# Expert slots' token numbers through a table in memory, and two other edits in the last pair of a one-layer diffusion backbone

## The reference, cut to what matters

```python
def hierarchical_moe(h, w_gr, b_gr, w_er, b_er, w_gate, w_up, w_down):
    ...
    e_val, e_idx = lax.top_k(e_in, TOP_K)                       # TOP_K = 2
    w_sel = jax.nn.softmax(e_val, axis=-1) * p_group
    ...
    y = jnp.zeros_like(h)
    for e in range(N_EXPERTS):                                  # 16 experts, hidden width 512
        he = jax.nn.silu(h @ w_gate[e]) * (h @ w_up[e])
        y = y + combine[:, e:e + 1] * (he @ w_down[e])
    return y
...
x = x + mod[5] * y.reshape(x.shape)
return rmsnorm(x, g_final)
```

## Time and profile before

| | us |
|---|---|
| median of 3 executions | 724.5 |
| lowest, highest | 723.94, 724.51 |
| the profiled execution, its own time | 724.15 |
| its span in the profile | 722.4 |

### The profile page before, as it was taken

One profiled execution on the slowest core, in us unless ns is written; L12 is line 12 of the kernel. 1 busy time (PEld: TensorE's weight loads), 2 busy tenths in 40 slices (PEclk: granted clock), 3 DMA queues, 4 the chain that ended last, 5 costly groups with the idle time before them and its releaser, 6 DMA issues.

```text
span 722.4 us, 7996 instructions
## 1 busy us (share of the span) xinstructions
PE 701.3 (97%) x3282; PEld 416.7 (58%) x3282; DVE 296.9 (41%) x507; ACT 112.2 (16%) x197; POOL 172.6 (24%) x126
## 2 busy tenths in 40 slices
PE   9999999999999999998999999999999999999995
PEld 5444586555775467776777788647434434443431
DVE  3439492778310475644343223325413212211315
ACT  4021011111000422221122230013000000000012
POOL 0008989789179000800000000000000000000010
PEclk9999999999999999999999999998999999999998
DMA  8994526762442332433481235995899999999991
GB/s 355 421 377 193 200 108 235 290 220 68 175 140 94 116 117 73 161 116 117 183 342 60 71 122 200 421 401 212 336 416 423 420 423 421 422 420 423 420 396 66
DMA packets 28933, 183.70 MB, mean 254 GB/s; under 512 B 3479, under 2 KB 5911, under 8 KB 13536
## 3 DMA queue, kind: packets, MB, share of 16 engines
q1 hardware_dynamic: 26880, 178.45, 62.4%
q0 software_dynamic: 1584, 3.97, 1.4%
q10 hardware_dynamic: 432, 0.75, 0.3%
HBM read 178.14 MB, written 6.82 MB: 256 GB/s over the span
## 4 chain that ended last, share of the span: by engine, by line
PE 91%; DMA 3%; DVE 2%; issue 2%; ACT 1%; SPq 0%; ACTq 0%; DVEq 0%; POOLq 0%
PE bank L1163 21%; PE bank L773 18%; PE bank L777 10%; PE bank L769 8%; PE bank L790 6%; PE bank L1116 4%; PE bank L995 4%; PE bank L796 4%; PE bank L920 2%; PE bank L941 2%; PE bank L822 2%; PE bank L928 2%; PE bank L783 2%; DMA y_rows<-sb,token_rows 1%; DMA sb<-y_rows 1%
## 5 line engine op out<-in xcount | busy, mean ns | idle before, releaser
L1163 PE MATMUL bank<-sb 128*64 128x512 f32 x768 | 167.5, 594 | 0.0
L773 PE MATMUL bank<-sb 128*128 128x256 f32 x576 | 128.5, 382 | 0.6 <-PE bank L769 0.3
L773 PEld LDWEIGHTS bank<-sb 128*128 128x128 f32 x576 | 108.1, 190 | 17.8 <-issue 3.8
L1163 PEld LDWEIGHTS bank<-sb 128*64 128x64 f32 x768 | 54.2, 137 | 106.7 <-issue 105.7
L565 POOL DMA_INDIRECT y_rows<-sb,token_rows x7 | 7.0, 997 | 371.5 <-DVE sb L1722 371.5
L525 POOL TENSOR_TENSOR sb<-sb 128x1024 f32<-128x1024 f32 x32 | 68.1, 2129 | 59.3 <-DMA sb<-ada_w 38.0
L1354 DVE COPY sb<-bank 128x512 f32<-128x512 f32 x45 | 29.2, 685 | 103.6 <-PE bank L928 66.2
L777 PE MATMUL bank<-sb 128*128 128x512 f32 x160 | 70.2, 593 | 0.3 <-PE bank L773 0.3
L769 PE MATMUL bank<-sb 128*128 128x512 f32 x128 | 55.8, 593 | 0.3 <-PE bank L995 0.3
L777 PEld LDWEIGHTS bank<-sb 128*128 128x128 f32 x160 | 29.9, 190 | 35.3 <-issue 35.3
L1687 DVE TENSOR_TENSOR sb<-sb,bank 128x512 f32<-128x512 f32 x8 | 5.5, 687 | 99.5 <-PE bank L1163 99.5
(11 more groups left out here) (246 smaller groups left out, 684.2 us busy)
## 6 DMA issues: line engine op xcount, KB each, us to landing
sb<-expert_w SPq DMA_DIRECT2D x94, 1024.0 KB, 19.3
sb<-front_w SPq DMA_DIRECT2D x19, 2048.0 KB, 8.1
sb<-ada_w SPq DMA_DIRECT2D x32, 512.0 KB, 3.5
sb<-ada_mix SPq DMA_DIRECT2D x4, 2048.0 KB, 20.4
sb<-xcT SPq DMA_DIRECT2D x4, 512.0 KB, 6.2
sb<-front_w SPq DMA_DIRECT2D x4, 512.0 KB, 21.1
y_rows<-sb SPq DMA_DIRECT2D x4, 512.0 KB, 23.2
sb<-expert_w SPq DMA_DIRECT2D x4, 512.0 KB, 5.6
```

What stands on the lines that cost most here:

```text
L773: ins = pe.matmul(ps[:, c * L:(c + 1) * L], lhs(w, k, (2 * i + c) * P), hT[:, k, 0:L], start=(k == 0), stop=(k == KD - 1))
L1163: ins = pe.matmul(bank[e * CAP:(e + 1) * CAP, :], lhsT[:, k, e * CAP:(e + 1) * CAP], weights_at(k, e), start=(k == 0), stop=(k == parts - 1))
```

## The change

**Token numbers by a table.** `tokens_of_slots` and `rows_of_tokens` are gone. In memory there is now a table `slot_tokens` of 896 integers, 7 for each of 128 partitions. DVE fills `token_rows` with 1024 at the very start, and POOL writes it out to the table. DVE works out, for each token and each of its two choices, the place of its slot in the table (`table_rows`, four columns; a place beyond the table if the choice has no slot there) and the number to be stored (`token_ids`). POOL then issues four indirect transfers of 128 single integers each, waits for them, reads the table back into `token_rows` and waits for that, all ahead of its loop over pairs. The constants `first_slot` and `token` are changed to match.

**Useless matmuls dropped.** `stay_warm` and its three uses are gone.

**The last pair's first half ahead of the rows.** On DVE, `experts_out(LAST, (0,))` now stands before all four `gathered_back` steps (it stood behind three of them), and `experts_out(LAST, (1,))` stands before `scaled_tokens` (it stood behind).

```diff
+            table = d["slot_tokens"].rearrange("(p n) o -> p (n o)", n=LAST)
+            pool.wait_ge(rows_unused, 1)
+            pool.dma_start(table, token_rows[:, :]).then_inc(table_cleared, 16)
+            pool.wait_ge(ids_ready, 2)
+            pool.wait_ge(table_rows_ready, 1)
+            pool.wait_ge(table_cleared, 16)
+            for q in range(2 * NT):
+                pool.indirect_dma_start(d["slot_tokens"][:, :], bass.IndirectOffsetOnAxis(table_rows[:, q:q + 1], 0),
+                                        token_ids[:, q:q + 1], None, bounds_check=STORED - 1, oob_is_err=False)\
+                    .then_inc(table_filled, 16)
+            pool.wait_ge(table_filled, 16 * 2 * NT)
+            pool.dma_start(token_rows[:, :], table).then_inc(token_rows_in, 16)
+            pool.wait_ge(token_rows_in, 16)
             pool.wait_ge(rows_cleared, 16 * 2 * NT)
             for n in range(LAST):
-                pool.wait_ge(token_rows_ready, 2 * n + 2)
                 pool.wait_ge(y_out, 2 * n + 2)
...
                     if q is not None and k % 4 == 0:
-                        if q == 6 * LAST + 2:
-                            stay_warm(1)
                         take_half(q + k // 4)
...
                 up(n, ring(6 * n + 2), 6 * n + 2)
                 if n < LAST:
-                    tokens_of_slots(n, S_now[n % 2])
-                if n < LAST:
                     gather(n + 1, S_now[(n + 1) % 2], (0,))
...
-                    if n == LAST and i == 0:
-                        stay_warm(2)
                     down(n, i, ring(6 * n + 4 + i), 6 * n + 4 + i)
...
+            dve.memset(token_rows[:, :], 1024).then_inc(rows_unused, 1)
             dve.memset(zeros, 0.0)
...
-                dve.scalar_tensor_tensor(out=token_of, in0=oh2, scalar=float(L),
-                                         in1=sm("token").unsqueeze(2).broadcast_to([P, NT, NE]), op0=ALU.mult, op1=ALU.add)\
-                   .then_inc(token_of_ready, 1)
+                link(dve.scalar_tensor_tensor(out=table_at, in0=slot_ok, scalar=-4096.0, in1=slot_at, op0=ALU.mult, op1=ALU.add))
+                dve.tensor_scalar(table_rows[:, :], table_at, 4096.0, None, ALU.add).then_inc(table_rows_ready, 1)
+                for j in range(2):
+                    dve.tensor_scalar(token_ids[:, NT * j:NT * j + NT], sm("token"), float(L * j), None, ALU.add)\
+                       .then_inc(ids_ready, 1)
...
                 modulate(n)
-                rows_of_tokens(n - 1)
...
             turned_out(LAST)
-            gathered_back(range(2 * NT - 1))
             experts_out(LAST, (0,))
-            gathered_back((2 * NT - 1,))
+            gathered_back(range(2 * NT))
             scattered(LAST, (0,))
+            experts_out(LAST, (1,))
             dve.wait_ge(glast_in, 16)
             dve.wait_ge(scat_out, NT)
             scaled_tokens()
-            experts_out(LAST, (1,))
             scattered(LAST, (1,))
```

More of the change, by code:

```diff
@@ L266, in build @@
         passes_f = keep(1)
-        slot_of, slot_ok = keep(32, NT, NE), keep(4)
-        slot_at, slot_w = keep(4), keep(4)
+        table_of, slot_ok = keep(32, NT, NE), keep(4)
+        slot_at, slot_w, table_at = keep(4), keep(4), keep(4)
         SW_now, ST_now = at(C0 + 6144, NT, P), at(C0 + 6144 + NT * P, NT, P)
@@ L282, in build @@
         token_rows = ctx.enter_context(nc.sbuf_tensor("token_rows", [P, LAST], I32))
-        token_of = keep(NT * NE, NT, NE)
+        token_ids = ctx.enter_context(nc.sbuf_tensor("token_ids", [P, 2 * NT], I32))
+        table_rows = ctx.enter_context(nc.sbuf_tensor("table_rows", [P, 2 * NT], I32))
         masks = ctx.enter_context(nc.sbuf_tensor("masks", [P, LEVELS - 1, P], I8))
@@ L1118, in gather @@
                     ins.then_inc(gather_ready, 1)
-            def tokens_of_slots(n, S):
-                pe.wait_ge(token_of_ready, 1)
-                if n:
-                    pe.wait_ge(token_rows_ready, 2 * n)
-                for t in range(NT):
-                    ins = pe.matmul(banks[7][:, 384 + 2 * n:386 + 2 * n], S[:, t, :], token_of[:, t, 2 * n:2 * n + 2],
-                                    start=(t == 0), stop=(t == NT - 1))
-                ins.then_inc(token_sum, 1)
             def ring(q):
@@ L1146, in retake @@
                     pe.wait_ge(w_in_[s], landed(q) - 16 * LAST + n * 16)
-            def stay_warm(n):
-                for _ in range(n):
-                    pe.matmul(banks[1][:, :], ident, small[:, 0:512], start=True, stop=True)
             def two_experts(bank, weights_at, parts, lhsT, q=None, n=None):
@@ L1705, in scattered @@
                         ins.then_inc(scat_out, 1)
-            def rows_of_tokens(n):
-                dve.wait_ge(token_sum, n + 1)
-                for e in range(2):
-                    part = slice(e * CAP, (e + 1) * CAP)
-                    dve.tensor_scalar(token_rows[part, n:n + 1], banks[7][part, 384 + 2 * n + e:385 + 2 * n + e], 1024.0, None,
-                                      ALU.add).then_inc(token_rows_ready, 1)
             def experts_out(n, halves=range(2)):
@@ L1738, in _ @@
             count_passes()
-            link(dve.tensor_tensor(slot_of, posm, sm("first_slot").unsqueeze(1).broadcast_to([P, NT, NE]), ALU.add))
+            link(dve.scalar_tensor_tensor(out=table_of, in0=posm, scalar=float(LAST),
+                                          in1=sm("first_row").unsqueeze(1).broadcast_to([P, NT, NE]), op0=ALU.mult, op1=ALU.add))
             choices()
@@ L1826, in shape_constants @@
     rank = np.arange(NE, 0, -1, dtype=f)
+    e = np.arange(NE)
+    first_row = np.where(e < 2 * LAST, e % 2 * CAP * LAST + e // 2 - LAST, 4096).astype(f)
     t = np.arange(L)
@@ L1956 @@
     d["y_rows"] = nc.dram_tensor("y_rows", (2 * L, D), F32).ap()
+    d["slot_tokens"] = nc.dram_tensor("slot_tokens", (STORED, 1), I32).ap()
     build(nc, d)
```

9 lines of the change are left out of this document (5 added, 4 removed).

## The result

| | before | after |
|---|---|---|
| median, us | 724.5 (5 executions) | 728.36 (5 executions) |
| lowest, highest | 723.94, 725.38 | 727.85, 729.57 |
| the profiled execution, its own time | 724.15 | 729.57 |
| its span | 722.4 | 727.3 |

The changed kernel is slower: the ratio is 1.0053, with a 95% interval of 1.0041 to 1.0064, so 3.9 us. The forecast was 720.4 and a range up to 723.2. The profiled execution of the changed kernel is the longest of its five, so its span exaggerates the loss by about one microsecond.

What follows compares the result with a forecast made beforehand. PE and the weight transfers were both full, with half 45's landing binding the last pair and DVE's additions the tail. A gain of 4.2 - 0.1 = 4.1 us from 724.15, plus 0.35, gave 720.4 us; range 718.9 to 723.2.

Steps and rivals of the forecast that it cites:

- Bounds: Expert part: two clocks, PE without a gap and weight transfers at 420 GB/s; which binds is read half by half.
- part 1: Small matmuls between `up` and the gather: removing them saves PE 0.47 us a pair, 3.3 us over seven pairs.
- the slack of 4.4 us: Last pair's `up`: how long before PE needed it half 45 landed; forecast to become 1.1 us late.
- Parts 2 and 3: Useless matmuls gone: `up` keeps 4.3 of 5.5 us, held by half 45's landing; down half 0 gains 0.9.
- Part 4: Table: DVE and POOL time covered; small packets take 0.4 us of the DMA engines, between nothing and 3.2 us.
- Part 5: DVE's order in the tail: `experts_out` of half 1 starts at 708.65 against 712.87, 4.2 us earlier.
- The sum: Whole kernel: 4.2 less 0.1 is 4.1 us earlier, profiled execution 720.05, median 720.4 us.
- B: Transfers cost more: table takes 3.2 us, or earlier `y_rows` reads delay half 46 or 47; up to 723.2; chance 0.20.
- C: PE's clock falls in the last pair: 723.9 with one slow half (chance 0.07), about 730 with both (0.04).
- A: Weights do not bind the last pair; PE runs at its own pace, at most 1.5 us more gained: 719.0; chance 0.13.
- D: Table over 11 us later than bounded, holding DVE in pair 1, or without effect: 724.5 or above; chance 0.06.

Runs made afterwards that it cites:

- at 512 bytes apart: Changed kernel, all three edits, with the table's integers 512 bytes apart instead of 4: 720.71 us against 725.12 for the kernel before, ratio 0.9922.
- the packed writes alone: Kernel before plus four indirect writes to an unused table, places 4 bytes apart: 732.62 us, ratio 1.0074; each write waited for: 731.24 us, ratio 1.0075.
- the reads held back: Changed kernel with integers 512 bytes apart, POOL also waiting for half 46 before reading `y_rows`: 723.7 us against 725.12 for the kernel before, ratio 0.9955.
- the one at 64 bytes: Changed kernel, all edits, with the table's integers 64 bytes apart instead of 4: 721.04 us against 724.64 for the kernel before, ratio 0.9951.

## Why the prediction was wrong

**Bounds, and part 1.** Right. PE's period fell from 25.41 to 24.96 us, 0.45 for the 0.47 expected. There were two clocks, and it was the other one, the weights, that decided; the slack of 4.4 us was read correctly.

**Parts 2 and 3.** The mechanism held: the end of the weights took the gain of PE. The size can be seen only where the stream isn't disturbed, at 512 bytes apart: 1.19 us of waiting (1.1 forecast), down half 0 at 697.78 (697.5 forecast). What released that half was, however, half 46 and not ACT's copy; the two fall within a microsecond of each other, and I had followed half 45 and half 47 but not half 46. That the useless matmuls may go is right too, for 1.2 us at the end (721.94 against 720.71).

**Part 4 is the step that failed.** It is the price of the table on the DMA engines. POOL's and DVE's time was covered, as said: the first transfer to `y_rows` was issued at 532.6. The price was taken as 0.4 us with 3.2 as its upper bound. It was 4.3 us by the bytes missing between 516 and 528, and 5.6 by half 45's landing (697.56 for 691.14, less 0.8 that the whole expert part started later in this execution). The bound came from queue 10 of the page of the profile, a mean over packets of other sizes and other work. The mistake was to treat a small packet as having a price of its own. With the same writes 64 or 512 bytes apart they cost nothing, and with the read back the table costs some 0.5 us, close to my 0.4; at 4 bytes it is beyond my bound. The count was off too: the trace has 160 packets in queue 0 (128 for the four writes, 32 for the read back) in place of 640, and as many at 512 bytes as at 4, so it is not the count that decides. Neither end was about the thing that mattered, which is where the bytes go. The row of a kind that I did not have was one of many writes into a few kilobytes, and no bound from rows that lack this can be called an upper one. That 0.4 fits the table at 512 bytes is luck: it was not chosen for a layout.

The Trainium skill, "DMA: Bandwidth & Descriptors", section Bandwidth, came nearer with its 10.5 ns a packet (an estimate of 6.7 us for 640 packets), but not for the right reason: by it the packets at 64 bytes apart would cost as much, and they cost nothing. For the 160 packets that the trace has, the same estimate is 1.7 us. The same page, section Specifications, says that transfers below 512 bytes are done as read-modify-write. If that alone made the stall, it would be there at 16 and 64 bytes apart as well; the runs show it at 4 bytes only. Whether it has a part in the stall at 4 bytes, no run here shows.

**Part 5.** The order of events was right: DVE went from the fourth addition to `scattered` to `experts_out` of half 1 without a wait, and the reads of `y_rows` were issued 3.3 us earlier (691.42 for 694.69). Two sizes were off. Half 47 was expected at 703 to 704 and the last read at 704 to 705; at 512 bytes apart down half 1 waits for half 47 until 705.15 and the last read lands at 706.51 (DVE waits 0.76 us ahead of the third addition), and in the changed kernel the same contention is added to the stall (the fourth read landed at 710.76, 17.6 us behind its issue, where it was 9.7). And in the changed kernel the clock fell under down half 0, 1.7 us.

**The sum again, for the profiled execution.** `experts_out` of half 1 started at 717.78, not at 708.65: 9.1 us later. Down half 0 began at 705.25 and not at 697.5, 7.75 of them: 0.8 from the front, some 5 from the table's stall, and the rest, 1.9, between the start of `up`'s second half and that of down half 0 (7.65 us for the forecast 5.8), where half 46 shares the engines with the reads. The low clock is 1.7, and DVE's strand was 0.35 shorter than I had put it. Behind `experts_out` nothing differs: 9.52 us to the end, 9.53 before. The last half microsecond lies outside the span, which leaves out 2.27 us of this execution and left out 1.75 before.

**The rivals.** B was the right one in kind, with both its mechanisms at once and a size outside its bounds; it ended at 723.2 because its price did. C came in as well, in its mildest form, 3.4 us long in the profiled execution; the others have no trace. In the kernel with the useless matmuls kept (the table alone, packed) down half 0 began as late, but PE had waited for weights 3.77 us in place of 7.65, with useless work in between, and its clock stayed up. One execution of each doesn't prove it, but this is what the useless matmuls were for. A and D were wrong. The interaction was missed altogether. The packed table alone costs 2.8 us, the other two edits alone gain 3.3, and together they cost 3.9 and not nothing: with the packed table down half 0 waits for half 46 either way (705.25 and 705.36), and what PE and DVE gain elsewhere is lost. And: without DVE's new order a table that costs nothing makes the kernel slower by 2.6 us, a fact that the parts, priced one by one, don't hold.

**What stays open.** What is held by the close integers on the way to memory wasn't found out, nor where between 4 and 16 bytes it begins, nor whether their distance or the size of the whole table decides. With the interval of each, the gain of the table at 512 bytes over the other two edits alone (720.71 against 722.09, on different chips, ratios 0.9922 and 0.9936) is not established. The spans of the profiled executions, 718.8 and 720.3, speak for it weakly, since 0.8 of the 1.5 us lies ahead of the first gate (505.22 and 506.05).

## What to carry to other kernels

The small scattered writes of this kernel are priced by where they land, not by how many they are: with 16 bytes or more from place to place they cost next to nothing. And when a transfer stream runs full, compare the megabytes that it moved in the stretch, before and after, since its engines look just as busy. Bytes lost early in a stream with a long backlog show up as waits much later, here 160 us, at the first place without slack. And an edit that brings one engine forward is worth nothing until the next thing in its line, here the addition that stood ahead of `experts_out`, is moved too.

## What the hardware showed that was not expected

- Indirect writes of 128 single integers, into places 4 bytes apart in a table of 3.5 KB, took the weights' stream from 422 to as little as 57 GB/s, and cost it 4.3 to 5.5 us for four writes (four kernels). At 16 bytes apart it was some 0.5 us by the bytes and nothing in the time, at 64 and 512 bytes nothing. In the stall the engines' busy share stays near 1 or above it for most of the time: the packets of the weights last longer (0.42 us for 0.28).
- The low level of the clock came under matmuls of the tail in five kernels: behind an idle time of PE of 4.95, 3.89 and 3.23 us ahead of scatter 0 (the table alone at 512 bytes, and the packed writes alone, four under way and one at a time), behind one of 2.94 us ahead of scatter 1 (the reads held back), and in the changed kernel under the half that followed waits of 2.02, 1.87 and 2.49 us. It cost 1.6 to 2.9 us. In the kernel at 512 bytes apart, whose longest idle times were 1.19, 1.04 and 1.33 us, it didn't come.
- In the router the clock is lowered in every profiled execution, but not for the same time: from 494 to 500 us the granted clock was 0.51 in the changed kernel and 0.72 in the one at 64 bytes, and the first gate started at 505.87 and 504.99. That is 0.9 us between two executions that have the same code there, as much as one of the edits is worth.
